# Sliding-window attention: exponentials multiplied by diagonal matrices of the inverse sums on TensorE

## The chip, the cores and the metric

The kernel runs on one core of a Trainium2 chip. The metric is the device time of one execution in microseconds (us); several executions of a kernel are timed and their median is taken. TensorE multiplies matrices, VectorE, ScalarE and GpSimd work element by element, and SyncE issues transfers. In the profile they are PE (with PEld for the loading of TensorE's stationary operand), DVE, ACT, POOL and SP.

## The reference

One layer of a hybrid decoder trunk runs over 1024 prompt tokens and 8 x 8 decode tokens. Its parts, in this order: a SwiGLU feed-forward half step with layer norm, a mixer, a layer norm, and a second feed-forward half step with layer norm. The mixer projects the input and runs two head groups side by side, retention (8 heads) and sliding-window attention (8 query heads in 2 key-value heads, window 128), and maps both by one output projection. Only the attention matters here:

```python
s = jnp.einsum('...qngd,...knd->...ngqk', qg, k) * HEAD_DIM ** -0.5
s = s - slopes * dist
s = jnp.where(valid, s, -jnp.inf)
m = jnp.maximum(jnp.max(s, axis=-1), sink)
p = jnp.exp(s - m[..., None])
denom = jnp.sum(p, axis=-1) + jnp.exp(sink - m)
o = jnp.einsum('...ngqk,...knd->...qngd', p / denom[..., None], v)
```

Each query attends to the keys of its own block of 128 and of the block before. The quotient `p / denom` has one divisor for each query and head.

## The kernel before

The program is a sequence of blocks, and each engine has its own queue of instructions in each block, written out by hand and joined by semaphores. A block begins when all engines have finished the block before. The blocks are: the first feed-forward with retention, the group norm and projection, the attention (`attention_stage`), and the output projection with the second feed-forward. A wait blocks everything behind it on the same engine.

The attention block works on 18 items, numbered 0 to 17: blocks of 128 tokens n = 0 to 7 and the decode tokens (n = 8), each for two key-value heads h. Item i is (n, h) with i = 2n + h. One item has four query heads and 256 keys, so 128 partitions (queries) by 1024 elements in the tile `at_scores`; items 0 and 1 have 128 keys only (512 elements), items 16 and 17 have 384 elements. There are four slots of `at_scores` and of `at_stats` (row maxima, sums and inverse sums), two of `at_turned`, but one pair of accumulator banks for the transposed scores.

For one item the engines do this:

- TensorE, `score_pair(n)` (line 1621): the products of queries and keys for both items of a token block. They have 64 rows, so two run side by side in the array's halves. Eight matrix products with 256 columns each stand as 16 records, since a product of full 32-bit floats is two records.
- VectorE, `add_bias` (line 1693) and `top` (lines 1701 to 1706): the scores are scaled, biased and written to `at_scores`, then the maximum is taken.
- ScalarE, `exponentials` (lines 1747 and 1749), which also gives the sums.
- VectorE, `denominator` (lines 1710 and 1712): the inverse sums.
- GpSimd (line 1808): all exponentials of the item are multiplied by the inverse sums, in place, and `normed` counts up.
- TensorE, `transposes(i)` (line 1642, lines 1635 and 1637 for the decode items): each 128 x 128 tile of the item is transposed into the banks `turn_ps`, eight of them (four in items 0, 1, 16 and 17). A transposition is one record, with the scores as stationary operand and the identity (`small`) as moving one.
- ScalarE, `read_turned` (line 1768): the banks are copied to `at_turned`.
- TensorE, `output(i)` (line 1663): the product with the values.
- ScalarE, `high_part` (line 1783), and VectorE, `low_part` (line 1727): the result is split into a high and a low part.

Beside this, ScalarE and GpSimd prepare the eight tiles of the output projection's weights: ScalarE rounds one (line 1508) at the end of each of its steps 0 to 7, and GpSimd takes the rest (line 1512) behind its items 1 to 8.

The orders of the queues:

```python
# TensorE
for i in range(LAST + 1):
    if i < LAST: transposes(i)
    if i % KVH == 0 and i + SLOTS < LAST: score_pair((i + SLOTS) // KVH)
    if i: output(i - 1)
# ScalarE
for i in range(LAST + 1):
    if i < LAST: read_turned(i)
    if i + SLOTS < LAST: exponentials(i + SLOTS)
    if i: high_part(i - 1)
    if i < KT: out_weights.round(act, i)
```

VectorE goes over `add_bias(i + 4)`, `top(i + 4)`, `denominator(i + 3)`, `low_part(i - 2)`. GpSimd goes over the normalisation of item i and then, for i from 1 to 8, `out_weights.split(i - 1)`, which waits for ScalarE's rounding of that tile.

Of the kernel before, what the change touches and what calls it, by code (L numbers as in the profile page):

```python
# [28 lines left out]
P = 128  # L29
# [6 lines left out]
DEC = DEC_BATCH * DEC_SEQ  # L36
# [4 lines left out]
GROUP = HEADS // KVH  # L41
# [1474 lines left out]
def attention_stage(core, at, at_caches, tables, sinks, sinks_dec, caches, q_t, k_t, v_tok, ident,  # L1516
# [9 lines left out]
    tag = "at_"  # L1526
# [5 lines left out]
    TOP, NEG, SUM, SINK, DEN, INV = range(6)  # L1532
    mc = Layout(core.nc, at_caches)
# [3 lines left out]
    v_cache = mc.put(tag + "v_cache", [P, DEC_BATCH, P])  # L1537
    turned_new = mc.put(tag + "turned_new", [P, 2 * P])
    q_rows = mc.put(tag + "q_rows", [P, DEC_BATCH, GROUP, DEC_SEQ])

    ITEMS = [(n, h) for n in range(BLOCKS + 1) for h in range(KVH)]
    LAST = len(ITEMS)
    KEYS = P + DEC
    sem = lambda n: core.semaphore(tag + n)
    score_ps, turn_ps, out_ps = [core.banks[0:2], core.banks[2:4]], core.banks[4:6], core.banks[6:8]
    bias_in = [sem(f"bias_in{h}") for h in range(KVH)]
    tables_in, dec_in, scored, biased, maxed, topped, negated, sink_exped, summed, inverted, \
        normed, turn_done, turn_read, out_done, hi_done, lo_done, stored, q_ordered = map(sem, (
            "tables_in", "dec_in", "scored", "biased", "maxed", "topped", "negated",
            "sink_exped", "summed", "inverted", "normed", "turn_done", "turn_read",  # L1550
            "out_done", "hi_done", "lo_done", "stored", "q_ordered"))

    def shape(i):

        n, h = ITEMS[i]
        if n == BLOCKS:
            return 2, 0, KEYS
        return GROUP, (P if n == 0 else 0), 2 * P

    def scores_of(i):  # L1560
        n, h = ITEMS[i]
        groups, k0, k1 = shape(i)
        width = KEYS if n == BLOCKS else 2 * P
        return scores[i % SLOTS][:, 0:groups * width].rearrange("p (g k) -> p g k", g=groups)[:, :, k0:k1]

    def per_group(i, what):
        return stats[i % SLOTS][:, what, 0:shape(i)[0]]
# [29 lines left out]
    def tensor(pe):  # L1597
        def score_pair(n):
            if n:
                pe.wait_ge(biased, KVH * n)  # L1600
            if n == BLOCKS:
                pe.wait_ge(dec_in, 32)
                pe.wait_ge(q_ordered, GROUP)
                for s in range(DEC_BATCH):
                    rows = slice(32 * (s % 4), 32 * (s % 4) + 32)
                    half = KEYS * (s // 4)
                    for h in range(KVH):
                        d = slice(HD * h, HD * h + HD)
                        q = q_rows[d, s, :, :].rearrange("p t i -> p (t i)")
                        pe.matmul(score_ps[h][0][rows, half:half + P], q, k_cache[d, s, :], start=True, stop=True)  # L1610
                        mm = pe.matmul(score_ps[h][0][rows, half + P:half + KEYS], q, k_t[d, SEQ:TOK],
                                       start=True, stop=True)
                        if s == DEC_BATCH - 1:
                            mm.then_inc(scored, 1)
            else:
                k0 = P if n == 0 else 0
                for t in range(GROUP):
                    col = 2 * P * (t % 2)
                    for h in range(KVH):
                        d = slice(HD * h, HD * h + HD)  # L1620
                        mm = pe.matmul(score_ps[h][t // 2][:, col + k0:col + 2 * P],
                                       q_t[d, t, P * n:P * n + P], k_t[d, P * (n - 1) + k0:P * (n + 1)],
                                       start=True, stop=True)
                        if t == GROUP - 1:
                            mm.then_inc(scored, 1)

        def transposes(i):
            n, h = ITEMS[i]
            pe.wait_ge(normed, i + 1)
            if i:  # L1630
                pe.wait_ge(turn_read, 2 * i)
            p = scores[i % SLOTS]
            if n == BLOCKS:
                for half in range(2):
                    pe.transpose(turn_ps[0][:, P * half:P * half + P], p[:, KEYS * half:KEYS * half + P], ident[:, :])
                for half in range(2):
                    mm = pe.transpose(turn_ps[1][0:DEC, P * half:P * half + P],
                                      p[:, KEYS * half + P:KEYS * half + KEYS], ident[:, :])
            else:
                for kb in range(1 if n == 0 else 0, 2):  # L1640
                    for t in range(GROUP):
                        mm = pe.transpose(turn_ps[kb][:, P * t:P * t + P],
                                          p[:, P * (2 * t + kb):P * (2 * t + kb) + P], ident[:, :])
            mm.then_inc(turn_done, 1)

        def output(i):
            n, h = ITEMS[i]
            d = slice(HD * h, HD * h + HD)
            pe.wait_ge(turn_read, 2 * i + 2)
            if i >= 2:  # L1650
                pe.wait_ge(lo_done, i - 1)
            if n == BLOCKS:
                for half in range(2):
                    mm = pe.matmul(out_ps[h][d, P * half:P * half + P], v_tok[:, BLOCKS, d],
                                   turned_new[:, P * half:P * half + P], start=True, stop=False)
                    for s in range(4 * half, 4 * half + 4):
                        col = slice(32 * s, 32 * s + 32)
                        mm = pe.matmul(out_ps[h][d, col], v_cache[:, s, d], turned[i % 2][0][:, col],
                                       start=False, stop=s % 4 == 3)
            else:  # L1660
                first = 1 if n == 0 else 0
                for kb in range(first, 2):
                    mm = pe.matmul(out_ps[h][d, :], v_tok[:, n - 1 + kb, d], turned[i % 2][kb][:, :],
                                   start=kb == first, stop=kb == 1)
            mm.then_inc(out_done, 1)

        for n in range(SLOTS // KVH):
            score_pair(n)
        for i in range(LAST + 1):
            if i < LAST:  # L1670
                transposes(i)
            if i % KVH == 0 and i + SLOTS < LAST:
                score_pair((i + SLOTS) // KVH)
            if i:
                output(i - 1)
# [122 lines left out]
    def gpsimd(pool):  # L1798
        for t in range(GROUP):
            pool.tensor_copy(q_rows[:, :, t, :], q_t[:, t, SEQ:TOK].rearrange("p (b i) -> p b i", i=DEC_SEQ))\  # L1800
                .then_inc(q_ordered, 1)
        pool.memset(turned_new[:, :], 0.0).then_inc(q_ordered, 1)
        for i in range(LAST):
            n, h = ITEMS[i]
            groups, k0, k1 = shape(i)
            pool.wait_ge(inverted, i + 1)
            s = scores_of(i)
            pool.tensor_tensor(s, s, per_group(i, INV).unsqueeze(2).to_broadcast([P, groups, k1 - k0]),
                               ALU.mult).then_inc(normed, 1)
            if 1 <= i <= KT:  # L1810
                out_weights.split(pool, i - 1)

    return Stage(sync=sync, tensor=tensor, vector=vector, scalar=scalar, gpsimd=gpsimd)


# [109 lines left out]
def decoder_layer(core, i, o):  # L1925
# [84 lines left out]
    with nc.Block() as block:  # L2010
# [48 lines left out]
        def _(pe):  # L2059
# [5 lines left out]
        core, att_end, mix_lo_att_at, gates_end, i["gn_sum"], i["gn_spread"], ones_head, eps, part("gn_w"), ret_q, ret_gate,  # L2065
        mix_hi, mix_lo, i["w_att"], xh, xl, ident, att_q, att_k, att_v_tok, retention.outputs_stored))
    one_stage_block(nc, attention_stage(core, att_end, mixer_at, i, part("sinks"), part("sinks_dec"),
                                        {"k": i["k_cache"], "v": i["v_cache"]}, att_q, att_k, att_v_tok, ident,
                                        mix_hi, mix_lo, o, out_weights))
# [202 lines left out]
```

## Time and profile before

| | us |
|---|---|
| Median of 3 executions | 2237.74 |
| Lowest and highest | 2236.16, 2239.15 |
| The profiled execution's own time | 2236.31 |
| Its span, first to last instruction | 2234.5 |

The span of the profile is the time from the first to the last instruction of that execution. In the lists of groups, the columns are line, engine, operation, tiles written and read, shapes and count, then busy us and mean ns of one, then idle us of the engine ahead of them with what ended it. In the timeline, the columns are start (us from the span's start), us from the first start to the last end of the merged records, engine, line, operation, tiles, shapes (128*64 is a stationary operand of 128 rows and 64 columns), count, and idle time ahead with its releaser. In the tables of stretches, the columns are the stretch, its length, TensorE's busy us with the count of its matrix records, the clock that TensorE was granted (1.00 is 2.4 GHz, 0.50 is 1.2 GHz), the share of the transfer engines, and GB/s.

### The profile page before, as it was taken

Reading aid. Unit: us, or ns where it says so; the run is one execution under the profiler, and the core shown is the slowest. Engines: PE = TensorE matmul, PEld = TensorE weight load, DVE = VectorE, ACT = ScalarE, POOL = GpSimd, SP = SyncE. Lnnn points to the kernel's source line nnn. Section 1 sums busy time; section 2 is a strip of 40 time slices with the busy share of each in tenths; the row PEclk is TensorE's granted clock in tenths of the full one; section 3 lists DMA queues with packets and bytes.
Section 4 is the critical chain, followed back from the end, with each engine's and each line's share of the span. In section 5 each row is a group of like instructions: output and inputs, shape, how many; then the busy total and the mean of one; then the engine's idle time right before and its main releaser. Section 6 shows DMA issues by size and latency. Waiting matters only on the chain. (4 is left out here: it accounts for less than half of the span.)

```text
span 2234.5 us, 31048 instructions
## 1 busy us (share of the span) xinstructions
PE 2139.6 (96%) x11989; PEld 1943.7 (87%) x11989; DVE 894.8 (40%) x1640; ACT 505.8 (23%) x869; POOL 519.8 (23%) x253
## 2 busy tenths in 40 slices
PE   8999999999999989999895689899999999999997
PEld 8999999999999979997674368899999999999996
DVE  5534344343434440015224433434343443434346
ACT  4111111111111341111224542311111111111115
POOL 4221211212122131213122512321212122121213
PEclk9999999999999999999897899999999999999999
DMA  7111010111101021110104030110110101011112
GB/s 275 42 43 56 28 56 28 56 45 39 56 28 57 31 79 51 44 38 25 67 10 141 1 118 1 38 48 31 54 56 28 56 28 56 28 56 41 43 57 81
DMA packets 38218, 118.43 MB, mean 53 GB/s; under 512 B 6407, under 2 KB 11015, under 8 KB 37903
## 3 DMA queue, kind: packets, MB, share of 16 engines
q1 hardware_dynamic: 38159, 117.61, 14.8%
q8 instruction: 41, 0.67, 0.1%
q14 instruction: 18, 0.15, 0.0%
HBM read 106.32 MB, written 11.27 MB: 53 GB/s over the span
## 5 line engine op out<-in xcount | busy, mean ns | idle before, releaser
L111 PE MATMUL bank<-x_hi,f_w_hi 128*128 128x362 f32 (+1 forms) x2104 | 688.4, 327 | 7.0 <-issue 5.6
L113 PE MATMUL bank<-x_hi,f_w_low 128*128 128x362 f32 (+1 forms) x2104 | 689.9, 328 | 0.0
L360 POOL TENSOR_TENSOR f_w_low<-f_w_raw,f_w_hi 128x1024 fp32r<-128x1024 f32 x132 | 317.3, 2419 | 1178.7 <-ACT f_w_hi L290 1178.7
L548 DVE TENSOR_TENSOR acc<-bank,acc 128x512 f32<-128x512 f32 x720 | 467.9, 686 | 7.1 <-PE bank L446 5.8
L111 PEld LDWEIGHTS bank<-x_hi,f_w_hi 128*128 128x128 f32 x2104 | 396.4, 188 | 9.2 <-issue 7.4
L526 DVE TENSOR_TENSOR f_h_full<-bank,f_silu 128x362 f32<-128x362 f32 (+1 forms) x132 | 70.7, 535 | 817.8 <-PE bank L113 815.6
L113 PEld LDWEIGHTS bank<-x_hi,f_w_low 128*128 128x128 f32 x2104 | 396.0, 188 | 0.0
L112 PE MATMUL bank<-x_lo,f_w_hi 128*128 128x362 f32 (+1 forms) x1056 | 345.3, 327 | 0.0
L112 PE MATMUL bank<-x_low,f_w_hi 128*128 128x362 f32 (+1 forms) x1048 | 342.9, 327 | 0.0
L444 PE MATMUL bank<-f_w_hi,f_h_hi 128*128 128x512 f32 x640 | 250.7, 392 | 0.3 <-DVE acc L548 0.3
L446 PE MATMUL bank<-f_w_low,f_h_hi 128*128 128x512 f32 x640 | 250.1, 391 | 0.0
L445 PE MATMUL bank<-f_w_hi,f_h_lo 128*128 128x512 f32 x640 | 249.9, 390 | 0.0
L299 ACT ACTIVATE f_silu<-bank 128x362 f32<-128x362 f32 (+1 forms) x132 | 62.5, 474 | 683.0 <-PE bank L113 683.0
L112 PEld LDWEIGHTS bank<-x_lo,f_w_hi 128*128 128x128 f32 x1056 | 199.0, 188 | 0.9
L112 PEld LDWEIGHTS bank<-x_low,f_w_hi 128*128 128x128 f32 x1048 | 197.2, 188 | 0.8
L305 ACT ACTIVATE f_h_hi<-f_h_full 128x362 fp32r<-128x362 f32 (+1 forms) x132 | 67.0, 508 | 528.9 <-DVE f_h_full L526 528.9
L446 PEld LDWEIGHTS bank<-f_w_low,f_h_hi 128*128 128x128 f32 x640 | 120.1, 188 | 26.7
L444 PEld LDWEIGHTS bank<-f_w_hi,f_h_hi 128*128 128x128 f32 x640 | 120.1, 188 | 25.2 <-DVE f_h_lo L534 0.6
L445 PEld LDWEIGHTS bank<-f_w_hi,f_h_lo 128*128 128x128 f32 x640 | 120.1, 188 | 24.6
L290 ACT ACTIVATE f_w_hi<-f_w_raw 128x1024 fp32r<-128x1024 f32 x132 | 134.0, 1044 | 32.5 <-DMA f_w_raw<-ffn_in 32.5
L111 PE MATMUL bank<-x_hi,rp_w_hi 128*128 128x362 f32 (+1 forms) x384 | 127.4, 332 | 3.9 <-ACTq L908 3.9
L113 PE MATMUL bank<-x_hi,rp_w_low 128*128 128x362 f32 (+1 forms) x384 | 126.5, 329 | 0.0
(195 smaller groups left out, 2247.4 us busy)
## 6 DMA issues: line engine op xcount, KB each, us to landing
f_w_raw<-ffn_in SPq DMA_DIRECT2D x132, 512.0 KB, 4.4
rp_w_raw<-w_ret_in SPq DMA_DIRECT2D x16, 512.0 KB, 3.5
acc<-x_rows_in SPq DMA_DIRECT2D x2, 2048.0 KB, 11.1
kept_rows<-acc SPq DMA_DIRECT2D x8, 512.0 KB, 2.9
ow_raw<-w_out_in SPq DMA_DIRECT2D x8, 512.0 KB, 10.5
y_out<-acc SPq DMA_DIRECT2D x8, 512.0 KB, 2.7
n_rows<-ln_rows_in SPq DMA_DIRECT2D x6, 512.0 KB, 8.3
gp_stage<-w_att_in SPq DMA_DIRECT2D x6, 512.0 KB, 3.5
```

What stands on the lines that cost most here:

```text
L111: pe.matmul(out, wh, xh, start=first, stop=False)
L112: pe.matmul(out, wh, xl, start=False, stop=False)
L113: return pe.matmul(out, wl, xh, start=False, stop=last)
L290: act.activation(flat(w_hi[s][j]), flat(w_raw[s][j]), ACT.Copy).then_inc(down_hi if j == DOWN else gu_hi, 1)
L299: act.activation(silu[:, buffer_of(f, s, c), 0:b - a], gate_ps[pair_of(f, s, c)][:, 0:b - a], ACT.Silu).then_inc(silu_done, 1)
L305: act.activation(h_hi[s][:, a:b], h_full[:, buffer_of(f, s, c), 0:b - a], ACT.Copy).then_inc(h_hi_done, 1)
L360: pool.tensor_tensor(flat(w_lo[s][j]), flat(w_raw[s][j]), flat(w_hi[s][j]).bitcast(F32), ALU.subtract).then_inc(done, 1)
L444: pe.matmul(out, h_hi[s][:, u], hi, start=True, stop=False)
L445: pe.matmul(out, h_lo[s][:, u], hi, start=False, stop=False)
L446: pe.matmul(out, h_hi[s][:, u], lo, start=False, stop=True).then_inc(down_done, 1)
L526: dve.tensor_tensor(h_full[:, at, 0:b - a], up_ps[pair_of(f, s, c)][:, 0:b - a], silu[:, at, 0:b - a], ALU.mult).then_inc(pair_free, 1)
L548: dve.tensor_tensor(acc[:, t, d], down_ps[(n + 2 * s) % 4][:, :], acc[:, t, d], ALU.add).then_inc(down_free, 1)
```

## The change

GpSimd no longer multiplies the exponentials. It makes one tile `at_diagonal` (two buffers, new), with 128 x 128 elements for each of the item's heads: the identity multiplied by the inverse sums of the queries, thus a diagonal matrix for each head. TensorE then multiplies each 128 x 128 tile of exponentials with its diagonal matrix, in a full matrix product, where it transposed before; the product with the diagonal matrix both transposes and normalises. GpSimd gets a wait: the diagonal of item i may be written when TensorE has done item i - 2.

```diff
@@ attention_stage
+    diagonal = [mc.put(f"{tag}diagonal{i}", [P, GROUP, P]) for i in range(2)]
@@ transposes(i)
             if n == BLOCKS:
                 for half in range(2):
-                    pe.transpose(turn_ps[0][:, P * half:P * half + P], p[:, KEYS * half:KEYS * half + P], ident[:, :])
+                    pe.matmul(turn_ps[0][:, P * half:P * half + P], p[:, KEYS * half:KEYS * half + P],
+                              diagonal[i % 2][:, half, :], start=True, stop=True)
                 for half in range(2):
-                    mm = pe.transpose(turn_ps[1][0:DEC, P * half:P * half + P],
-                                      p[:, KEYS * half + P:KEYS * half + KEYS], ident[:, :])
+                    mm = pe.matmul(turn_ps[1][0:DEC, P * half:P * half + P],
+                                   p[:, KEYS * half + P:KEYS * half + KEYS], diagonal[i % 2][:, half, :],
+                                   start=True, stop=True)
             else:
                 for kb in range(1 if n == 0 else 0, 2):
                     for t in range(GROUP):
-                        mm = pe.transpose(turn_ps[kb][:, P * t:P * t + P],
-                                          p[:, P * (2 * t + kb):P * (2 * t + kb) + P], ident[:, :])
+                        mm = pe.matmul(turn_ps[kb][:, P * t:P * t + P],
+                                       p[:, P * (2 * t + kb):P * (2 * t + kb) + P], diagonal[i % 2][:, t, :],
+                                       start=True, stop=True)
@@ gpsimd(pool)
             pool.wait_ge(inverted, i + 1)
-            s = scores_of(i)
-            pool.tensor_tensor(s, s, per_group(i, INV).unsqueeze(2).to_broadcast([P, groups, k1 - k0]),
+            if i >= 2:
+                pool.wait_ge(turn_done, i - 1)
+            pool.tensor_tensor(diagonal[i % 2][:, 0:groups, :], ident[:, :].unsqueeze(1).to_broadcast([P, groups, P]),
+                               per_group(i, INV).unsqueeze(2).to_broadcast([P, groups, P]),
                                ALU.mult).then_inc(normed, 1)
```

## Rows read from the trace of the kernel before

**Rows 1.** Head of the page: the span, and the busy time of TensorE.
```profile
span 2234.5 us, 31048 instructions
PE 2139.6 (96%) x11989; PEld 1943.7 (87%) x11989; DVE 894.8 (40%) x1640; ACT 505.8 (23%) x869; POOL 519.8 (23%) x253
```

**Rows 2.** Table of stretches, TensorE: the attention block, bursts and gaps in it, what follows.
```profile
1186.50:1310.00 123.50, 78.85 (x420) 0.83 0.18 64
...
1233.10:1239.40 6.30, 6.30 (x25) 0.50 0.00 0
...
1244.80:1250.10 5.30, 0.00 (x0) 0.96 0.00 0
...
1267.10:1270.10 3.00, 2.97 (x14) 0.50 0.00 0
...
1281.00:1304.00 23.00, 20.61 (x144) 1.00 0.00 1
1312.10:1317.90 5.80, 5.80 (x14) 0.50 1.00 407
```

**Rows 3.** Waits of the attention block: who waited for whom, us in total, times, longest.
```profile
POOL ow_low L1512 <- ACT ow_hi L1508: 36.4, 7, 10.1
PEld bank L1642 <- POOL at_scores L1808: 29.3, 6, 9.0
```

**Rows 4.** Timeline of all engines, 1233 to 1251 us: one cycle.
```profile
1233.09 1.97 PE L1642 MATMUL bank<-small,at_scores 128*128 128x128 f32 x8 [5.34 <-POOL at_scores L1808]
...
1234.98 3.79 PE L1621 MATMUL bank<-att_k,att_q 64*128 64x256 f32 x16
...
1238.70 2.29 PE L1663 MATMUL bank<-at_turned,att_v_tok 128*64 128x512 f32 x4
...
1241.91 0.51 ACT L1747 ACTIVATE at_scores<-at_scores,at_stats 128x256 f32<-128x256 f32 x1 [5.73 <-DVE at_stats L1706]
...
1244.72 1.06 ACT L1508 ACTIVATE ow_hi<-ow_raw 128x1024 fp32r<-128x1024 f32 x1
...
1245.85 2.35 POOL L1512 TENSOR_TENSOR ow_low<-ow_raw,ow_hi 128x1024 fp32r<-128x1024 f32 x1 [8.24 <-ACT ow_hi L1508]
...
1248.16 1.90 POOL L1808 TENSOR_TENSOR at_scores<-at_scores,at_stats 128x1024 f32<-128x1024 f32 x1
...
1250.11 1.97 PE L1642 MATMUL bank<-small,at_scores 128*128 128x128 f32 x8 [5.34 <-POOL at_scores L1808]
```

**Rows 5.** Groups by form: GpSimd's normalisation, the full items and items 0, 1.
```profile
L1808 POOL TENSOR_TENSOR at_scores<-at_scores,at_stats 128x1024 f32<-128x1024 f32 x14 | 26.5, 1892 | 12.1 <-DVE at_stats L1712 12.1
...
L1808 POOL TENSOR_TENSOR at_scores<-at_scores,at_stats 128x512 f32<-128x512 f32 x2 | 2.1, 1041 | 11.9 <-DVE at_stats L1712 11.9
```

**Rows 6.** TensorE's timeline, items 8 to 15, in the same block.
```profile
1267.13 1.97 PE L1642 MATMUL bank<-small,at_scores 128*128 128x128 f32 x8 [5.34 <-POOL at_scores L1808]
...
1271.51 1.93 PE L1663 MATMUL bank<-at_turned,att_v_tok 128*64 128x512 f32 x4
...
1278.76 1.06 PE L1642 MATMUL bank<-small,at_scores 128*128 128x128 f32 x8 [1.18 <-ACT at_turned L1768]
1279.75 2.00 PE L1621 MATMUL bank<-att_k,att_q 64*128 64x256 f32 x16
1281.68 1.93 PE L1663 MATMUL bank<-at_turned,att_v_tok 128*64 128x512 f32 x4
...
1292.98 1.09 PE L1642 MATMUL bank<-small,at_scores 128*128 128x128 f32 x8
1294.00 1.93 PE L1663 MATMUL bank<-at_turned,att_v_tok 128*64 128x512 f32 x4
```

**Rows 7.** TensorE's last instruction in the attention block.
```profile
1307.68 0.60 PE L1658 MATMUL bank<-at_turned,at_v_cache 128*64 128x32 f32 x8
```

**Rows 8.** TensorE's timeline in retention: full 32-bit products, 128 columns, whole array.
```profile
1032.91 0.49 PE L1166 MATMUL bank<-rt_q_dec,rt_state 128*128 128x128 f32 x2
1033.33 0.44 PE L1155 MATMUL bank<-rt_probs,ret_v_tok 128*64 128x128 f32 x4
```

## The prediction

> **What bounds the kernel now.** I began with the page's head. TensorE is busy 96% of the span of 2234.5 us [rows 1], so over the whole program GpSimd's time is worth nothing; the question is the attention block alone. The table of stretches shows that block (1186.5 to 1310.0) as an exception: TensorE is busy 78.85 of 123.5 us there, at a mean granted clock of 0.83 [rows 2]. So something else sets the pace in it, for a part of the time.
>
> The waits of the block name it: TensorE's line 1642 waited 29.3 us for GpSimd's line 1808, and GpSimd's line 1512 waited 36.4 us for ScalarE's line 1508 [rows 3]. One cycle of the timeline gives the whole chain [rows 4]. Transpositions of item 4 start at 1233.09, the score products at 1234.98, and they are done at 1238.70. VectorE adds the bias and takes the maximum until ScalarE's exponentials start at 1241.91. These and the high part run until 1244.72, the rounding of a weight tile takes 1.06, GpSimd's split of it 2.35 from 1245.85, and its normalisation of item 6 takes 1.90 from 1248.16. Transpositions of item 6 start at 1250.11, after 5.34 us in which TensorE stood still. The cycle is 17.02 us. GpSimd's normalisation is on it because the split stands ahead of it in the same queue; all else that the odd item needs runs beside it. This cycle stands three times (starts of items 2, 4 and 6; item 8 starts 17.02 after item 6 [rows 4, 6]), and item 2 itself waits for a normalisation in the same way.
>
> From item 8 on GpSimd has no split left and is ahead. Item 10's transpositions wait for ScalarE to empty the banks, and in items 12 to 17 TensorE's instructions stand back to back: 20.61 us busy of 23.0 at full clock [rows 2, 6]. There TensorE sets the end of the block, and the next block starts after it.
>
> **The clock.** The burst from 1233.10 to 1239.40 ran at 0.50 of the clock (1.2 GHz); the burst at 1267.10 ran at 0.50 until 1270.10 only, and what follows from 1281 had 1.00 (2.4 GHz) [rows 2]. Ahead of each TensorE had stood idle for 5.3 us [rows 4, 6]. So the rise came 3.1 to 6.4 us after a burst's start, in the same kind of work. A burst is an even item's transpositions and the score products, and took 5.61 us with the late rise [rows 4] and 4.38 with the early one [rows 6].
>
> **The parts.** GpSimd: half as many elements. The normalisation of 1024 elements took 1892 ns, that of 512 took 1041 [rows 5]. The diagonal tile has 4 x 128 = 512 elements and the same operation with a broadcast operand, so 1.04 us: 0.85 less, on the chain for items 2, 4, 6 and 8: **-3.4 us**. Bounds: nothing if the second broadcast operand costs what was saved. For other items and for the wait added nothing: item i's diagonal waits for item i - 2's products, and behind it in GpSimd's queue is a split; at item 4 the transpositions of item 2 are 12 us old, and in items 12 to 17 each diagonal may start one whole item (about 3 us [rows 6]) before its use and takes 1.04. VectorE's maximum of item i + 4 waits for that diagonal and is itself not late by then. The buffer, SyncE and the transfers don't change.
>
> TensorE: each transposition is one record, each full product two. No row has this very shape in a stream. The nearest: the score products are 16 records of 256 columns, two side by side, so eight steps of 256, the same columns as 16 steps of 128. They took 1.93 us at full clock [rows 6] and 3.72 at half [rows 4]. Eight transpositions took 1.02 from start to next at full clock [rows 6] and 1.89 at half [rows 4]. I take 1.97 for the 16 new records, and 3.8 at half clock: +0.95 and +1.9 an item. Lower bound +0.7 (the fixed part hidden), upper bound from a product of the exact shape that stands alone in retention: 0.42 us for two records [rows 8], eight of which are 3.36, so +2.34. I take the stream's value, since there the next operand is loaded while the last one is used, and the same shape follows itself here.
>
> Bursts of items 2, 4, 6, 8: at half clock 3.8 + 3.72 = 7.52. With a rise at 3.1 us: 3.1 + 4.42 / 2 = 5.3; at 6.4: 6.4 + 1.12 / 2 = 7.0; in the middle (4.75) 6.1, against 5.2 before for the same rise (4.75 + 0.86 / 2). So +1.0 each (0.9 to 1.35): **+4.0**.
>
> Items 10, 12, 13, 14, 15, full clock, on the path: 5 x 0.95 = **+4.75**. Items 16 and 17 have four tiles each, half of it: 2 x 0.45 = **+0.9**. Items 0 and 1 have slack before the next scores. Odd items up to 11: their transpositions come when ScalarE isn't ready for them, so nothing; without that cover they are 5 x 0.95 = 4.75 more.
>
> Sum: -3.4 + 4.0 + 4.75 + 0.9 = **+6.2 us**. Against the profiled execution's 2236.3 it is a little less: three of its four bursts had the late rise, 21.2 us in all, and middle bursts of 6.1 make 24.6, so +3.4 in place of +4.0; and the next block began with at least 5.8 us at half clock [rows 2], where a middle rise gives back half of 1.1. That makes 2236.3 + 5.1 = 2241.4. The median stands 1.4 above that execution, and its bursts will have been nearer the middle, so I put the like-for-like 6.2 on the median: 2237.7 + 6.2 = **2243.9 us**.
>
> **Two rules of the Trainium skill.** A full product here costs about twice a transposition by the rows: 16 steps in 1.93 against 8 in 1.02 [rows 6]. "TensorE: Matmul & The Clock Gate", in Terms, says that transpose mode is 4x faster for FP32. By that rule the eight products would take 4 x 1.02, an estimate of 4 us at full clock, and the sum would be near that of the first rival; retention's lone product, 0.42 against 0.13, is no proof of it, as it includes the filling of the array.
>
> The clock did rise in bursts that hold transpositions, after 3.1 us in the one of item 8 [rows 2, 6]. The same page, in Part 4, says that a transposition doesn't count as activity for the clock as a matmul does. By that rule real products would bring the rise sooner or keep the clock up: the second rival.
>
> **The rivals.** First, the full price: each product costs the 0.42 us of [rows 8], whether by load or by passes. Tail 5 x 2.34 = 11.7, items 16 and 17 +2.2, bursts 6.7 + 3.7 at half clock with a middle rise 7.6 each, so +9.7 over four, less 3.4: +20, 2258 us. For it: the exact shape. Against: every stream of such records in the trace has the columns' price. Chance 0.09.
>
> Second, faster: TensorE's gap before items 4, 6 and 8. It is 5.3 us, of which the clock fell only at the end (0.96 over the gap [rows 2]). The chain behind the scores shrinks by 0.85 and the odd item's products grow into the gap, so it comes to 4.5. If the clock then holds, three bursts take 1.97 + 1.93 = 3.9 against 5.2: -1.3 each, while item 2's keeps +1.0. Sum: -3.4 + 1.0 - 3.9 + 5.65 = -0.7; and if it also holds over the 3.8 us between the last product and the next block's first [rows 2, 7], 2.4 (half of a middle rise) less: -3.1, 2234.6. It decides from the point where the gap is too short for a fall; the one fall that I can date came in the last 0.5 us of 5.3, so 4.5 is near. For it also the greater activity. Against: the clock was at half after that shorter pause of 3.8 us too. Chance 0.15, a third of it below -4.5 in the runs' scatter.
>
> Third, the diagonal costs GpSimd as much as the normalisation did: +9.6, 2247.3. Chance 0.07. Fourth, rises come early in all bursts of the new kernel (5.3 each): +2.5 to +3, 2240.5. Chance 0.12.
>
> **How the numbers follow.** The forecast has 0.57. Its own range is +3.5 to +9, from the records' price (0.7 to 1.2 an item) and the rise in four bursts. The range of all, 2237.5 to 2249.5, leaves out the full price and the lower part of the clock's rival. About 0.2% (4.5 us) is what a measurement can tell from no change. Slower by more: 0.44 of the forecast's 0.57, the first and third rival 0.16, some of the fourth: 0.62. Faster by more: 0.05. The rest, 0.33, is within.
>
> **What would show it.** Line 1808's successor: 14 instructions at about 1.04 us more, 16 in all. Records of the products: 240 in full items for 120, 16 in 1.97 us at full clock. Starts of items 2, 4, 6 and 8 at 1215.2 and then about 17.2 apart. Items 12 to 16 take 3.8 us more. The block ends 5 to 6 us later. Wrong would be: 16 records in over 3 us, a granted clock of 1.00 from the start of items 4, 6 and 8, or a wait of GpSimd's new wait that TensorE then waits for.

## The result and the profile after

| us | before | after |
|---|---|---|
| Median (lowest to highest) | 2236.89 (2235.73 to 2239.15), 7 runs | 2244.41 (2240.02 to 2245.55), 7 runs |
| The profiled execution's own time | 2236.31 | 2242.74 |
| Its span | 2234.5 | 2241.0 |

The ratio is 1.0029, with a 95% interval of 1.0018 to 1.0041: the change costs 4 to 9 us. 2243.9 was forecast. One execution, of the version with four diagonal tiles below, took 5441 us and is used nowhere.

The head of the page after, to be held against [rows 1]:

```profile
span 2241.0 us, 31320 instructions
PE 2157.0 (96%) x12117; PEld 1964.8 (88%) x12117; DVE 898.4 (40%) x1640; ACT 506.2 (23%) x869; POOL 508.0 (23%) x253
```

GpSimd has 12 us less to do and TensorE 17 us more. Neither number is the result; the attention block has to be read for that. Its table of stretches after, TensorE's columns as in [rows 2]:

```profile
1186.50:1316.00 129.50, 94.95 (x548) 0.83 0.17 61
1214.30:1219.90 5.60, 5.60 (x26) 0.50 0.01 3
1231.40:1237.00 5.60, 5.57 (x24) 0.50 0.00 0
1244.80:1248.50 3.70, 0.00 (x0) 0.83 0.00 0
1248.50:1254.00 5.50, 5.47 (x24) 0.50 0.00 0
1265.60:1271.10 5.50, 5.49 (x24) 0.50 0.00 0
1271.20:1304.00 32.80, 29.92 (x221) 1.00 0.00 1
1318.00:1322.30 4.30, 4.27 (x10) 0.50 0.94 387
```

All four bursts (items 2, 4, 6, 8) begin at half clock and keep it for 5.5 to 5.6 us. In the gap before item 6 the clock has already fallen (0.83 over 3.7 us).

The waits of the block after. The first line is the split's wait of [rows 3], the second the wait that the change adds, and the third TensorE's wait for the exponentials, now for the diagonal:

```profile
POOL ow_low L1512 <- ACT ow_hi L1508: 41.7, 8, 9.2
...
POOL at_diagonal L1813 <- PE bank L1645: 28.4, 7, 5.0
...
PEld bank L1645 <- POOL at_diagonal L1813: 23.5, 6, 5.7
```

TensorE's timeline after: the first burst that compares with [rows 4], items 8, 12, 14 and the next block's first product:

```profile
1231.43 3.78 PE L1645 MATMUL bank<-at_diagonal,at_scores 128*128 128x128 f32 x16 [4.49 <-POOL at_diagonal L1813]
1235.14 2.90 PE L1622 MATMUL bank<-att_k,att_q 64*128 64x256 f32 x16
...
1265.61 3.78 PE L1645 MATMUL bank<-at_diagonal,at_scores 128*128 128x128 f32 x16 [4.49 <-POOL at_diagonal L1813]
...
1290.51 2.02 PE L1645 MATMUL bank<-at_diagonal,at_scores 128*128 128x128 f32 x16 [1.18 <-ACT at_turned L1772]
1295.52 2.05 PE L1645 MATMUL bank<-at_diagonal,at_scores 128*128 128x128 f32 x16
1297.50 1.93 PE L1667 MATMUL bank<-at_turned,att_v_tok 128*64 128x512 f32 x4
...
1318.03 0.77 PE L1865 MATMUL bank<-ow_hi,mix_hi 128*128 128x512 f32 x1 [3.82 <-DVEq L1879]
```

An item's 16 records take 1.98 us from their start to the next instruction's (1295.52 to 1297.50), where eight transpositions took 1.02 [rows 6]; at half clock 3.71 (1231.43 to 1235.14), where they took 1.89. The 5.34 us in which TensorE stood still have become 4.49. And the groups by form hold GpSimd's new line, 1041 ns where [rows 5] had 1892:

```profile
L1813 POOL TENSOR_TENSOR at_diagonal<-small,at_stats 128x512 f32<-128x512 f32 x16 | 16.6, 1041 | 34.3 <-PE bank L1645 22.4 <-DVE at_stats L1716 11.9
```

The added time can be followed from start to start, in the two profiled executions:

| stretch, by the starts of TensorE's items | before | after | added |
|---|---|---|---|
| to item 2 | 1216.07 | 1214.29 | -1.78 |
| item 2 to item 8 | 51.06 | 51.32 | +0.26 |
| item 8 to item 10 | 11.63 | 13.77 | +2.14 |
| item 10 to item 12 | 10.17 | 11.13 | +0.96 |
| item 12 to item 16 | 12.74 | 16.53 | +3.79 |
| item 16 to the next block's first product | 10.43 | 10.99 | +0.56 |
| the next block's first product at | 1312.10 | 1318.03 | +5.93 |

In this execution the three cycles of 17 us come out as long as before, since each gives 0.85 and takes 0.93 back. The tail, where TensorE is the bound, pays in full.

### The profile page after: what moved, and what is told of

Read it like the earlier page. It is cut to its first block and busy times, and to the rows that moved or that the text cites. A ratio compares the mean times of both kernels' runs of the same rounds, so it can differ in the third digit from the quotient of the medians.

```text
span 2241.0 us, 31320 instructions
## 1 busy us (share of the span) xinstructions
PE 2157.0 (96%) x12117; PEld 1964.8 (88%) x12117; DVE 898.4 (40%) x1640; ACT 506.2 (23%) x869; POOL 508.0 (23%) x253
## 5 line engine op out<-in xcount | busy, mean ns | idle before, releaser
L445 PEld LDWEIGHTS bank<-f_w_hi,f_h_lo 128*128 128x128 f32 x640 | 120.2, 188 | 24.6
## 6 DMA issues: line engine op xcount, KB each, us to landing
acc<-x_rows_in SPq DMA_DIRECT2D x2, 2048.0 KB, 11.3
```

Of the source, the lines that this page charges most:

```text
L445: pe.matmul(out, h_lo[s][:, u], hi, start=False, stop=False)
```

## The experiments

The time of the block was read as the distance of its first product from the next block's: 125.4 us before, 131.35 after. The changed kernel profiled a second time gave 130.2, and the version with the products alone gave 134.3 and 132.2, so a single value is good to about 2 us. The block's own start lies between 1184.9 and 1190.0 from one profiled execution to the next with the same code ahead of it. Small differences are therefore read from medians.

### The halves of the change

Products with the identity in place of the transpositions, in all three calls (one is shown, shortened), and GpSimd's normalisation kept:

```diff
-    mm = pe.transpose(turn_ps[kb][...], p[...], ident[:, :])
+    mm = pe.matmul(turn_ps[kb][...], p[...], ident[:, :], start=True, stop=True)
```

> The kernel before with TensorE's half of the change alone: full products with the identity in place of the transpositions, GpSimd's normalisation stays. My theory (prices add up: bursts of items 2 to 8 +4.0, items 10 and 12 to 17 +5.65, nothing back from GpSimd) gives +9.6 us, 2246.5, and item starts 4, 6, 8 some 18 us apart. Rival (the longer burst brings the clock's rise into it and so pays for part of itself): +6 to +7.5, 2243 to 2244.5, starts 17.5 apart or less. If the sum of this run and of the diagonal alone is not the whole change's +7.5 within 1.5 us, the halves don't add.

Measured: 2244.04 against 2237.84, ratio 1.0027 (1.0016 to 1.0039). One burst and what follows in its timeline:

```profile
1250.30 3.78 PE L1643 MATMUL bank<-small,at_scores 128*128 128x128 f32 x16 [5.34 <-POOL at_scores L1810]
1254.01 2.31 PE L1621 MATMUL bank<-att_k,att_q 64*128 64x256 f32 x16
...
1267.67 3.78 PE L1643 MATMUL bank<-small,at_scores 128*128 128x128 f32 x16 [5.34 <-POOL at_scores L1810]
```

The products cost what they cost with diagonals (3.71 us to the next instruction), the gap is the old 5.34, and the cycle is 17.37 here and 17.67 and 18.24 for the two before it: longer than 17.02 in all three. But the +6.2 us are the rival's figure and not the +9.6 of the plain sum; taken again below, the same version gave +8.9.

GpSimd's diagonal alone: written as in the change, with its wait, and read by nobody. The transpositions stay, and the normalisation of the attention's output is left out. The edit, shortened:

```diff
-            pool.tensor_tensor(s, s, per_group(i, INV)..., ALU.mult).then_inc(normed, 1)
+            if i >= 2:
+                pool.wait_ge(turn_done, i - 1)
+            pool.tensor_tensor(diagonal[i % 2][:, 0:groups, :], ident[...], per_group(i, INV)..., ALU.mult).then_inc(normed, 1)
```

> The kernel before with GpSimd's half of the change alone: it writes the diagonal tiles and has the new wait, TensorE transposes the exponentials as before and doesn't use the diagonals, so the attention's output is left unnormalised (that part of the computation is left out). My theory: 0.85 us less on the chain at items 2, 4, 6, 8, so -3.4 us, 2233.5, starts 16.2 apart. Rival A (the new wait or the split eats it): 0, 2237. Rival B (starts closer together also keep TensorE's clock up, so it gains more than its own time): -5 us, 2232, with the granted clock above 0.80 in the cycles of items 4 and 6.

Measured: 2232.61 against 2237.84, ratio 0.9979 (0.9970 to 0.9988), 4.7 us less by the ratio. Its timeline:

```profile
1229.37 1.97 PE L1643 MATMUL bank<-small,at_scores 128*128 128x128 f32 x8 [4.49 <-POOL at_diagonal L1810]
1231.27 3.74 PE L1622 MATMUL bank<-att_k,att_q 64*128 64x256 f32 x16
...
1245.50 1.97 PE L1643 MATMUL bank<-small,at_scores 128*128 128x128 f32 x8 [4.49 <-POOL at_diagonal L1810]
```

The cycle is 16.1 (1229.37 to 1245.50), 0.9 below 17.02, and the gap is 4.49. So the shorter operation shortens the chain by about its own difference. The time is that of rival B, but its sign is hardly there: the granted clock over the cycles of items 4 and 6 is 0.82 and 0.80, for 0.80 in both before. The bursts of items 4 and 6 still ran at half clock although TensorE stood still for less; that of item 8 had full clock for its first half microsecond.

The products alone and the whole change, both unaltered, were then timed beside each other, to see whether the halves add up.

> TensorE's half of the change alone once more (full products with the identity, GpSimd's normalisation kept), beside the run before. Theory: 2.5 to 3.5 us slower than the changed kernel, 2246 to 2248. Rival: the same within 1 us, 2243.5 to 2245.

> The changed kernel once more, beside the next one on the same chip. The whole change measured +7.5 us, its halves alone +6.2 and -5.2. If the halves add (theory of the sum, -3 us for GpSimd's part inside the whole change), this is 2.5 to 3.5 us below the run with the products alone. If GpSimd's saving is given back inside the change, by the new wait or by VectorE's one delayed addition (2.2 us in place of 0.16, seen at item 5), both are within 1 us of each other.

Measured: products alone 2245.65, ratio 1.0039 (1.0025 to 1.0053); the change 2240.79, ratio 1.0024 (1.0015 to 1.0033). They are 4.9 us apart, where halves that add were expected to give 2.5 to 3.5 and the rival less than 1. The rival falls.

The first timings had said otherwise: +6.2 and -5.2 for the halves make +1.0, and the change had measured +7.5, further off than the 1.5 us that had been set as the limit. In the second timing the change itself is at +4.1. Over all executions of the study the medians are 2237.3 before (50 executions), 2244.8 with the products alone (12), 2232.6 with the diagonal alone (11) and 2242.2 with the change (18). So +7.5 and -4.7 stand against +4.9 for both. The halves act against each other, as the sum had them. Whether they add exactly stays open: +2.8 and +4.9 are 2.1 us apart, and the change's own two timings are 3.4 apart.

### The new wait

Four diagonal tiles in place of two (also `i % 4` for `i % 2` at every use, not shown), so that GpSimd waits for item i - 4:

```diff
-    diagonal = [mc.put(f"{tag}diagonal{i}", [P, GROUP, P]) for i in range(2)]
+    diagonal = [mc.put(f"{tag}diagonal{i}", [P, GROUP, P]) for i in range(4)]
-            if i >= 2:
-                pool.wait_ge(turn_done, i - 1)
+            if i >= 4:
+                pool.wait_ge(turn_done, i - 3)
```

> The changed kernel with four diagonal tiles instead of two, so that GpSimd's new wait falls on item i - 4 instead of i - 2. GpSimd waited 28.4 us for TensorE in the changed kernel. My theory: each diagonal was ready at least one item before its use, so this wait costs nothing and the time stays within 1 us of the changed kernel (2243 to 2245.5), with item starts as there. Rival: diagonals made late are on the path or push the splits behind them, and the time falls by 2 to 4 us.

Measured: 2243.1 over six executions against 2237.57, ratio 1.0030 (1.0018 to 1.0042), as the change itself; the block 131.5 us. GpSimd's wait for line 1645 is gone from the list of waits, and what TensorE waits for has stayed:

```profile
POOL at_diagonal L1813 <- DVE at_stats L1716: 36.0, 9, 7.3
...
PE bank L1645 <- POOL at_diagonal L1813: 17.6, 4, 4.5
```

The last row was 17.7 with two tiles. The 28.4 us of the new wait were worth nothing: GpSimd waited there for a buffer where it otherwise waits for the sums (36.0 us here, 11.9 with two tiles).

### The clock and transpositions

In items 2, 4, 6 and 8 of the kernel before, each transposition four times over (32 in a burst), so that a rise can fall among transpositions alone.

```diff
-                for kb in range(1 if n == 0 else 0, 2):
+                for kb in [kb for _ in range(4 if i in (2, 4, 6, 8) else 1) for kb in range(1 if n == 0 else 0, 2)]:
```

> The kernel before, with the eight transpositions of items 2, 4, 6 and 8 done four times over (same result), so that a burst begins with 32 transpositions, some 6.8 us of them at half clock. Theory: transpositions count as work for the clock, so it rises within them, 3.1 to 6.4 us after the burst's start, as in the other bursts. Rival, the rule of the Trainium skill (TensorE: Matmul & The Clock Gate, Part 4): they don't count, the clock stays at half through all 32 and rises 3 us or more after the score products begin, 10 us or more after the burst's start.

One profiled execution (2246.36 us). The timeline of the first burst, then the stretches of the first and third with the granted clock:

```profile
1215.77 5.88 PE L1642 MATMUL bank<-small,at_scores 128*128 128x128 f32 x32 [6.88 <-POOL at_scores L1808]
```

```profile
1215.80:1220.20 4.40, 4.40 (x21) 0.50 0.02 4
1220.30:1221.50 1.20, 1.20 (x13) 1.00 0.00 0
1254.70:1257.70 3.00, 2.99 (x14) 0.50 0.02 5
1257.90:1259.80 1.90, 1.90 (x19) 1.00 0.00 0
```

The clock rose after 4.5, 5.8, 3.1 and 5.1 us of nothing but transpositions. This goes against the rule of the Trainium skill that the prediction weighed ("TensorE: Matmul & The Clock Gate", Part 4), and the measurement decides. And the rise came anywhere from 3.1 to 5.8 us after the start of the same work.

### Where the block's bound lies

The prediction's chain says that GpSimd waits for ScalarE's rounding, which stands behind the exponentials. So the rounding was put ahead of them, in the kernel before and in the changed one:

```diff
+            if i < KT:
+                out_weights.round(act, i)
             if i + SLOTS < LAST:
                 exponentials(i + SLOTS)
             if i:
                 high_part(i - 1)
-            if i < KT:
-                out_weights.round(act, i)
```

> The kernel before, with ScalarE's rounding of the weight tile ahead of the exponentials in its steps 0 to 7 instead of at their end. If GpSimd's work is on the chain only because the split ahead of it waits for that rounding (my theory), items 4, 6 and 8 no longer wait for GpSimd, their starts come 10 to 11.5 us apart instead of 17.0, the gaps of 5.3 us and the half clock go, and the time falls by 20 to 26 us, to 2211 to 2217. Rival (ScalarE is the limit in these steps, 4.9 us of work an item, or GpSimd's own 4.25 us an item): -3 to -8 us.

> The changed kernel with the same move. GpSimd's cheaper work is then off the chain and worth nothing, so by my theory the change costs its whole price on TensorE: slower than the kernel before with the same move by 6 to 9 us (0.96 an item on the path in at least items 8, 10, 12 to 15, half of it in 16 and 17), 2218 to 2226. Rival (GpSimd's 0.85 us an item matter more once the cycle is short): no slower than the other, 2211 to 2217.

Measured: before with the rounding first 2225.82, ratio 0.9949 (0.9934 to 0.9964); the changed kernel with it 2228.27, ratio 0.9956 (0.9941 to 0.9971). The gain is real and large, and it misses the 2211 to 2217 that was expected. The change on top costs 2.4 us by the medians, where 6 to 9 were expected; the intervals of the two ratios overlap, so these runs can't tell 2.4 from nothing (the block is 113.5 and 115.2 us). The timeline of VectorE and GpSimd in the first of them shows what was overlooked:

```profile
1232.02 2.35 POOL L1512 TENSOR_TENSOR ow_low<-ow_raw,ow_hi 128x1024 fp32r<-128x1024 f32 x1 [0.23 <-ACT ow_hi L1508]
1232.78 1.61 DVE L1703 TENSOR_TENSOR at_stats<-at_stats,small 128x4 f32<-128x4 f32 x1
1234.33 1.89 POOL L1808 TENSOR_TENSOR at_scores<-at_scores,at_stats 128x1024 f32<-128x1024 f32 x1
1234.42 1.81 DVE L1705 TENSOR_TENSOR at_stats<-small,at_stats 128x4 f32<-128x4 f32 x1
1236.16 0.16 DVE L1706 TENSOR_SCALAR at_stats<-at_stats 128x4 f32<-128x4 f32 x1
```

Two VectorE instructions on 4 elements a partition, 0.16 us each elsewhere, end exactly when GpSimd's running instruction ends: 1234.39 beside 1234.37, and 1236.23 beside 1236.22. They make the exponentials 3 us late, and the cycle is 13.7, where 10 to 11.5 was expected. In the changed kernel with the rounding first the second one is shorter, as GpSimd's is:

```profile
1235.29 1.08 DVE L1707 TENSOR_TENSOR at_stats<-at_stats,small 128x4 f32<-128x4 f32 x1
1236.31 1.03 POOL L1813 TENSOR_TENSOR at_diagonal<-small,at_stats 128x512 f32<-128x512 f32 x1
1236.40 0.96 DVE L1709 TENSOR_TENSOR at_stats<-small,at_stats 128x4 f32<-128x4 f32 x1
```

0.96 in place of 1.81: there the shorter operation of GpSimd gives 0.85 a second time, on VectorE's way to the exponentials, which fits the small cost of the change in this setting. The Trainium skill has the rule, in "SBUF — State Buffer", "SBUF: two separate sides": VectorE and GpSimd share a port pair by an exclusive lock, held for a whole instruction; VectorE takes it in its two-port modes, and for two inputs in SBUF against a GpSimd operation that reads SBUF. The rows agree: 1.81 us for what takes 0.16, to the end of GpSimd's instruction.

To try it, the two instructions with two inputs were each written as four with one input and a scalar operand for each partition, in the kernel before with the rounding first:

```diff
-            dve.tensor_tensor(per_group(i, TOP), per_group(i, TOP), sinks_of(i), ALU.max).then_inc(topped, 1)
+            for g in range(shape(i)[0]):
+                x = dve.tensor_scalar(per_group(i, TOP)[:, g:g + 1], per_group(i, TOP)[:, g:g + 1],
+                                      sinks_of(i)[:, g:g + 1], None, ALU.max)
+            x.then_inc(topped, 1)
...
-            dve.tensor_tensor(per_group(i, SINK), sinks_of(i), per_group(i, TOP), ALU.subtract)
+            for g in range(shape(i)[0]):
+                dve.tensor_scalar(per_group(i, SINK)[:, g:g + 1], sinks_of(i)[:, g:g + 1],
+                                  per_group(i, TOP)[:, g:g + 1], None, ALU.subtract)
```

> The kernel before with the rounding first, and with VectorE's two additions of an item (maximum with the sinks, difference to the sinks) written as one instruction for each head with one tensor and one scalar for each partition, in place of two tensors of 4 elements; the splits stay on GpSimd. Theory (only VectorE instructions with two tensors in SBUF are shut out while GpSimd runs one): the delays of 1.6 and 1.8 us go, the instructions take some 0.1 to 0.2 us each beside GpSimd, pairs of items come 11.5 to 12.5 us apart in place of 13.7, and the time is 2214 to 2221 against 2225.8. Rival (every VectorE instruction of that place waits for GpSimd): the first of them still takes over 1 us, and the time stays at 2224 to 2228.

Measured: 2221.83 against 2236.72, ratio 0.9933 (0.9918 to 0.9948), just outside the 2214 to 2221 expected. Its timeline:

```profile
1233.41 2.35 POOL L1512 TENSOR_TENSOR ow_low<-ow_raw,ow_hi 128x1024 fp32r<-128x1024 f32 x1 [0.23 <-ACT ow_hi L1508]
1234.06 0.58 DVE L1704 TENSOR_SCALAR at_stats<-at_stats,small 128x1 f32<-128x1 f32 x4
1234.67 0.58 DVE L1709 TENSOR_SCALAR at_stats<-small,at_stats 128x1 f32<-128x1 f32 x4
1235.16 0.62 DVE L1711 TENSOR_SCALAR at_stats<-at_stats 128x4 f32<-128x4 f32 x1
```

The eight small instructions run in the middle of GpSimd's split, so in this form they weren't held up. But the hold-up went to the next instruction, the last line above, with one input of four elements: 0.62 us here, to the end of the split at 1235.76. Over the whole block it looks so (ns, least, median and most):

```profile
L1711 DVE TENSOR_SCALAR at_stats<-at_stats x18: 156/159/2186, 1192.2 to 1281.4; 128x4 f32<-128x4 f32 x16, 128x2 f32<-128x2 f32 x2
```

It took 1.02, 2.19, 1.88, 0.62 and 0.92 us in five of its 18 places, each time to the end of GpSimd's instruction. So two inputs aren't needed for the hold-up. The edit changed two things at once, the number of inputs and that of elements, and which of them freed the eight instructions isn't shown; nor was it tried whether the same section's two-port modes are the reason for the last line's. By the ratios the edit is worth 3.6 us over the rounding alone (0.9933 and 0.9949 of 2237), with intervals that overlap; the expected 11.5 to 12.5 us for a pair of items came out as 11.0 to 12.2 from item 4 on.

### The split taken from GpSimd

Rounding first, and the weights' low parts computed on VectorE in place of GpSimd, in the kernel before and in the changed one:

```diff
# VectorE, after low_part(i - 2)
+            if 0 <= i < KT:
+                out_weights.split(dve, i)
# GpSimd
-            if 1 <= i <= KT:
-                out_weights.split(pool, i - 1)
```

> The kernel before, with the rounding ahead of the exponentials and the low part of the weight tiles made on VectorE (at the end of its iterations 0 to 7), not on GpSimd. In the run with the rounding first alone, VectorE's additions of 4 elements with two inputs in SBUF took 1.6 and 1.8 us in place of 0.16, each until GpSimd's instruction ended. Theory (GpSimd and VectorE exclude each other on such instructions): with the split gone from GpSimd, such a delay is at most one normalisation of 1.9 us an item, the pairs of items come 11 to 12.5 us apart instead of 13.7, and the time falls another 4 to 8 us, to 2218 to 2222. Rival (VectorE's additional 1.1 us an item is itself on the chain): no gain, 2224 to 2228.

> The changed kernel with both moves. Theory: GpSimd then has only 1.04 us an item, so it seldom meets VectorE's additions, and what is left of the change is TensorE's price of 0.96 us an item on the path: 4 to 8 us slower than the kernel before with both moves, 2223 to 2229. Rival (the shorter instruction on GpSimd pays for TensorE's price by way of VectorE, as it nearly did with the first move alone, where the difference was 2.5 us): within 2.5 us of each other.

Measured: the kernel before with both edits 2212.49, ratio 0.9897 (0.9882 to 0.9912); the changed kernel with both 2220.75, ratio 0.9925 (0.9910 to 0.9940). Both are faster than expected (2218 to 2222 and 2223 to 2229). The first is the fastest of the study, some 23 to 25 us below the kernel before and about 30 below the changed one. VectorE and GpSimd in its timeline:

```profile
1234.61 2.30 DVE L1512 TENSOR_TENSOR ow_low<-ow_raw,ow_hi 128x1024 fp32r<-128x1024 f32 x1
...
1240.31 3.38 POOL L1810 TENSOR_TENSOR at_scores<-at_scores,at_stats 128x1024 f32<-128x1024 f32 x1 [4.49 <-DVE at_stats L1712]
1240.72 1.21 DVE L1512 TENSOR_TENSOR ow_low<-ow_raw,ow_hi 128x1024 fp32r<-128x1024 f32 x1
...
1244.03 1.06 PE L1642 MATMUL bank<-small,at_scores 128*128 128x128 f32 x8 [1.18 <-ACT at_turned L1770]
```

VectorE does the split in 1.21 us (GpSimd took 2.35), and in 2.30 in the first row, where GpSimd's normalisation ran until 1235.82. The hold-up works both ways: GpSimd's normalisation, 1.89 alone, takes 3.38 around VectorE's split, although the rows have it start 0.41 us sooner. But TensorE now waits for ScalarE's reading of the banks (1.18), not for GpSimd, the cycle is 11.3, and TensorE's pauses from item 2 on are 2.3 us at most. The stretches of the two kernels, first the one without the change, then the one with it:

```profile
1234.30:1288.80 54.50, 41.52 (x279) 1.00 0.02 3
```

```profile
1213.10:1294.90 81.80, 71.17 (x483) 1.00 0.01 3
```

From 1234.3 and from 1213.1 on the clock holds at 1.00, through items that began at half clock before. In this setting the change costs 8.3 us by the medians and 6.3 by the ratios, where 4 to 8 were expected: GpSimd isn't on the path, so its saving is worth nothing, and 4.4 us come from item 12 on, where each item takes 0.95 more. The block as a whole is only 3.5 us longer in the two profiled executions (103.6 and 107.2), as what stands ahead of item 12 takes 0.8 us less; most of the rest of the distance between these two is the block's own start (1185.0 and 1190.0), with the same code ahead of it.

## Why the prediction was right

**The bound.** Right. TensorE's 16 to 17 us cycle follows GpSimd's chain: 0.85 less in GpSimd's operation took 0.9 from the cycle with nothing else changed, and moving the rounding forward took 12 us from the kernel. That GpSimd is busy for only 23% said nothing about it.

**GpSimd's operation.** Right. -0.85 in each of four items was forecast, 1041 ns with two broadcast operands measured. The diagonal alone was worth 4.7 us in the medians, for 3.4 forecast. The third rival, no saving, falls.

**The products.** Right. 1.97 at full and 3.8 at half clock were forecast from the score products' stream, 1.98 and 3.71 measured. Items 12 to 16 took 3.79 more, for 3.8. The lone product of retention (0.42) was the wrong row to price a stream by, and the full-price rival falls. The Trainium skill's factor of 4 for transpose mode ("TensorE: Matmul & The Clock Gate", Terms) is 1.98 to 1.02 here, 1.9 in a stream, and the measurement decides.

**Odd items and items 16 and 17.** Nothing was forecast for the odd items up to 11, and their longer products did grow into a pause: in the cycle of item 4 TensorE's wait ahead of the next output product fell from 0.85 us to 0.26, and item 10 to 12 took only one item's 0.96 more. For items 16 and 17 +0.9 was forecast, +0.56 came in this profile.

**The bursts.** This is the term that was off in the profiled execution. A middle rise was assumed, 6.1 us a burst and 24.6 for four. All four rises came late, 5.5 to 5.6 us after the start, and the bursts took 6.58, 6.54, 6.52 and 6.52: 26.2. Against the profile before that is +5.0, for +3.4 forecast. The same kernel profiled again, in an execution of 2239.6 us, had earlier rises:

```profile
1213.33 3.75 PE L1645 MATMUL bank<-at_diagonal,at_scores 128*128 128x128 f32 x16 [6.67 <-POOL at_diagonal L1813]
...
1218.94 1.07 PE L1667 MATMUL bank<-at_turned,att_v_tok 128*64 128x512 f32 x2
```

Its bursts took 5.61, 6.01, 6.26 and 6.38, 24.3 in all, as forecast, and its cycles 16.16, 16.56 and 16.81, shorter than the 17.02 before. The one execution with 32 transpositions a burst shows the rise from 3.1 to 5.8 us for the same work. So it is scatter and no property of the change, and whether a cycle of the changed kernel gains or only breaks even is a matter of it.

What made up for it: item 2 began 1.78 earlier, not 0.85, as the score products ahead of it (1201.79) had full clock for their first microsecond and took 2.78 in place of 3.68 (3.58 in the later profile, so this is scatter too). The next block started 5.93 later, for 5.65 forecast, and kept half clock for 4.3 us in place of 5.8 or more. The remaining 1.3 of the span's 6.5 lie in the second feed-forward, whose code is the same. That the profiled execution came out near its forecast is partly luck, because these offset each other. So is it that the median fell within 0.5 us of 2243.9: the second timing of the same kernel gave 2240.79, and over all executions the change costs 4.9 us, for 6.2 forecast. That is inside the forecast's own range (+3.5 to +9), and barely above the 4.5 us that the prediction took for the limit of what can be told.

**The clock's rival.** The gap shrank to 4.49 us as forecast, and the clock fell in each; before item 6 it was 0.83 over the last 3.7 us. With real products it fell all the same, and with transpositions it rose all the same. In the version with the split on VectorE it held from 1234.3 on, with pauses of up to 2.3 us. But no length of a pause decides it in these runs. In the same version the clock fell (0.53 from 1230.7) one microsecond into the products behind an earlier pause of 2.3 us; in the one-input version it held behind one pause of 2.44 us (1.00 from 1236.8) and was at 0.50 behind another (from 1248.6); in the changed kernel with the rounding first it fell at 1239.4, soon after a pause of 2.0; and with the diagonal alone it was 1.00 through the last 4.4 us before item 8.

**The new wait.** Forecast at nothing; with it taken away nothing changed.

**What it missed.** VectorE and GpSimd hold each other up. The profile before has no such case. The changed kernel has one, ahead of item 2:

```profile
1210.90 2.34 POOL L1512 TENSOR_TENSOR ow_low<-ow_raw,ow_hi 128x1024 fp32r<-128x1024 f32 x1 [9.23 <-ACT ow_hi L1508]
1211.06 2.20 DVE L1707 TENSOR_TENSOR at_stats<-at_stats,small 128x4 f32<-128x4 f32 x1
1213.20 1.04 POOL L1813 TENSOR_TENSOR at_diagonal<-small,at_stats 128x512 f32<-128x512 f32 x1
1213.29 0.96 DVE L1709 TENSOR_TENSOR at_stats<-small,at_stats 128x4 f32<-128x4 f32 x1
```

3.2 us for two instructions of 0.16, once. The later profile of the same kernel shows none, and the second one with the products alone, where GpSimd still normalises, shows one of 2.11 and 1.82 us; so it doesn't come from the diagonal. The cycle behind it is as long as the next two (17.14, 17.10, 17.08), so its price in the changed kernel is nothing that can be seen; it matters in the versions with the rounding first.

## What to carry to other kernels

Moving work from a lightly used engine to the one that sets the end pays only where the light engine's instruction is itself a link of the chain, and only as often as it is one: here four of 18 items gained 0.85 us, while each item on TensorE's path paid 0.95 at full clock. Look first at what that link waits for: GpSimd was late because ScalarE's rounding stood behind the exponentials, and moving two lines was worth 12 us, moving the split to VectorE some 12 more by the ratios. Price an instruction by a stream of its kind, and let the clock's rise have the whole range that traces show.

## What was unexpected in the hardware

- VectorE's operations and GpSimd's hold each other up for whole instructions: a 4-element maximum with two inputs in SBUF took up to 2.20 us in place of 0.16, a multiplication of one input of four elements up to 2.19 in place of 0.16, and GpSimd's normalisation 3.38 in place of 1.89. Written with one input of one element and a scalar, the maximum ran beside GpSimd at 0.58 us for four.
- The rise of TensorE's clock came 3.1 to 5.8 us after the start of the same work, in transpositions alone too. It fell within or soon after every pause of 3.0 us and more in the timelines of this block (0.83 over the last 3.7 us of one of 4.49, and only half a microsecond behind another of 4.49). Behind pauses of 2.0 to 2.4 us it held in some places and fell in others.
- VectorE took 1.21 us for the subtraction that takes GpSimd 2.35 (128 x 1024 elements).
- A full 32-bit product of 128 columns costs two records, 0.12 us each at full clock in a stream (1.98 for 16), and 1.9 times a transposition.
